# The samples' values of a cross-attention, with the probabilities as the stationary operand in four column groups

## The reference

```python
qh = q.reshape(bsz, t, H_C, DH_C)                 # 4 heads of 128
s = jnp.einsum('bthd,bmhd->bhtm', qh, mem_k) * (DH_C ** -0.5)
p = jax.nn.softmax(s, axis=-1)
o = jnp.einsum('bhtm,bmhd->bthd', p, mem_v).reshape(bsz, t, D_C)
y_c = o @ w_c_out
...
merged = g[:, :, 0] * y_a + g[:, :, 1] * y_b + g[:, :, 2] * y_c
```

## Time and profile before

| | us |
|---|---|
| median of 3 runs | 1988.23 (1987.68 to 1988.99) |
| the profiled execution | 1984.89 |
| its span, first to last instruction | 1983.1 |
| TensorE busy | 1878.6 |
| VectorE busy | 1482.1 |
| ScalarE busy | 1066.3 |
| GpSimd busy | 136.5 |

### The profile page before, as it was taken

The page is one execution under the profiler, slowest core; times in us unless marked ns, Lnnn a source line. Parts: engine busy times, 40 slices in busy tenths (PEclk is TensorE's granted clock), DMA queues, the critical chain, the costliest instruction groups (busy, mean ns, idle before and its releaser), DMA issues.

```text
span 1983.1 us, 28034 instructions
## 1 busy us (share of the span) xinstructions
PE 1878.6 (95%) x10353; PEld 1604.9 (81%) x10354; DVE 1482.1 (75%) x2119; ACT 1066.3 (54%) x1206; POOL 136.5 (7%) x159
## 2 busy tenths in 40 slices
PE   7999999899998999999889999999999999999993
PEld 7899899799987989899766678888888888886672
DVE  6997686755536999667576668888888888886665
ACT  4452754543324444474444456767777776765442
POOL 1110000000001020000020001020202020201000
PEclk9999999899999999999989999999999999999997
DMA  7553344344443563444456569898989898996522
GB/s 268 203 215 143 138 151 144 109 168 149 149 141 116 191 229 136 149 149 150 149 211 250 199 233 339 335 382 331 374 331 380 337 375 333 366 346 241 210 106 87
DMA packets 118613, 446.91 MB, mean 225 GB/s; under 512 B 10384, under 2 KB 10384, under 8 KB 118016
## 3 DMA queue, kind: packets, MB, share of 16 engines
q1 hardware_dynamic: 112288, 424.45, 58.1%
q0 software_dynamic: 6240, 21.33, 3.2%
HBM read 435.68 MB, written 12.67 MB: 226 GB/s over the span
## 4 chain that ended last, share of the span: by engine, by line
PE 42%; issue 3%; DVE 3%; ACT 1%; DMA 1%; SPq 0%; DVEq 0%; POOLq 0%; POOL 0%; ACTq 0%
PE psum L1996 11%; PE psum L1997 11%; PE psum L1998 11%; PE psum L2003 3%; PE psum L2002 3%; ACT wph L616 1%; PE psum L1736 1%; PE psum L2059 1%; DVE wpl L622 1%; DVE hT L1674 0%; DMA x<-out_acc 0%; DMA out_acc<-arena,rows_out 0%; DVE arena L1663 0%; PE psum L2062 0%; DVE x L1164 0%
## 5 line engine op out<-in xcount | busy, mean ns | idle before, releaser
L622 DVE TENSOR_TENSOR wpl<-e_ring,wph 128x2048 fp32r<-128x2048 f32 x269 | 606.9, 2289 | 85.5 <-ACT wph L616 84.5
L616 ACT CAST wph<-e_ring 128x2048 fp32r<-128x2048 f32 x269 | 501.7, 1903 | 119.6 <-PE psum L1998 66.7
L574 DVE TENSOR_TENSOR wl<-ring,wh 128x1024 fp32r<-128x1024 f32 x234 | 285.3, 1223 | 208.1 <-ACT wh L568 207.4
L1750 PE MATMUL psum<-xTh,wh 128*128 128x320 f32 x1184 | 375.3, 317 | 31.6 <-DVE xTl L1266 11.0
L1751 PE MATMUL psum<-xTl,wh 128*128 128x320 f32 x1184 | 369.9, 312 | 0.0
L1752 PE MATMUL psum<-xTh,wl 128*128 128x320 f32 x1184 | 369.7, 312 | 0.0
L568 ACT CAST wh<-ring 128x1024 fp32r<-128x1024 f32 x234 | 243.9, 1046 | 138.6 <-PE psum L1771 71.2
L1996 PE MATMUL psum<-wph,xe 128*128 128x512 f32 (+1 forms) x768 | 293.6, 382 | 2.8 <-issue 2.4
L1997 PE MATMUL psum<-wph,xe 128*128 128x512 f32 (+1 forms) x768 | 289.1, 376 | 0.0
L1998 PE MATMUL psum<-wpl,xe 128*128 128x512 f32 (+1 forms) x768 | 288.7, 376 | 0.0
L1750 PEld LDWEIGHTS psum<-xTh,wh 128*128 128x128 f32 x1184 | 225.7, 191 | 40.0 <-DVE wl L574 15.7
(11 more groups left out here) (327 smaller groups left out, 2528.5 us busy)
## 6 DMA issues: line engine op xcount, KB each, us to landing
e_ring<-experts SPq DMA_DIRECT2D x264, 1024.0 KB, 6.4
ring<-stream SPq DMA_DIRECT2D x274, 512.0 KB, 3.2
lnp<-rows POOLq DMA_DIRECT2D x4, 1024.0 KB, 6.1
x<-x POOLq DMA_DIRECT2D x3, 512.0 KB, 5.8
arena<-x0T SPq DMA_DIRECT2D x2, 640.0 KB, 5.9
o_a<-arena POOLq DMA_DIRECT2D x2, 540.0 KB, 7.6
o_k<-arena POOLq DMA_DIRECT2D x2, 512.0 KB, 7.0
o_v<-arena POOLq DMA_DIRECT2D x2, 512.0 KB, 8.8
```

The source lines that it names most:

```text
L574: dve.tensor_tensor(wl[:, q % SPLITS, :], ring[:, u % SLOTS, :], wh[:, q % SPLITS, :].bitcast(F32), ALU.subtract).then_inc(lo_done, 1)
L616: act.copy(wph[:, SLOT_OF[m % NPOS], :], ring_place(m).rearrange("p u c -> p (u c)")).then_inc(hi_e, 1)
L622: dve.tensor_tensor(wpl[:, s, :], ring_place(m).rearrange("p u c -> p (u c)"), wph[:, s, :].bitcast(F32), ALU.subtract).then_inc(lo_e, 1)
L1750: pe.matmul(out, h[:, k], hi[:, k], start=(k == 0), stop=False)
```

## The change

The values of four samples are made together. The stationary operand is now the 32 columns of probabilities of one sample (4 heads x 8 tokens) and the moving operand the 512 columns of its values; the four samples go to four groups of 32 partitions of one bank (`ob`). ScalarE copies that bank to SBUF (`obs`), and four transposes, one for each head, turn it into a bank `ot`, from which only the blocks on the diagonal (the head's own rows) are copied into `oTh` and subtracted into `oTl`. The four banks `o` now hold the prompt alone. A list `ATTEND` gives the order of the stretch: ob0, g0, g1, ot0, g2, g3, ob1, g4, mean, g5, ot1, g6, g7, var. The stream in memory is as before; `stands_at` tells where each unit stands in it.

```diff
-MEAN_AFTER = 2
+ATTEND = [("ob", 0), ("g", 2, 0), ("g", 2, 1), ("ot", 0), ("g", 2, 2), ("g", 2, 3), ("ob", 1), ("g", 2, 4),
+          ("mean", 0), ("g", 2, 5), ("ot", 1), ("g", 2, 6), ("g", 2, 7), ("var", 0)]
+MEAN_AFTER = 4
...
+        for n, key in enumerate(ATTEND):
+            p.tile(l, *key, bank=others[n % 4])
+        p.step([(l, "o", h) for h in range(H_C)])
+        for key in ATTEND:
+            if key[0] == "ob":
+                for n in range(4):
+                    p.step([(l, *key)] if n == 3 else [], (l, "cv", 4 * key[1] + n))
+            elif key[0] == "g":
+                p.step([(l, *key)], (l, *key), split=True)
+            else:
+                p.step([(l, *key)])
...
                 for n in range(H_C):
                     made(l, "o", n)
-                    act.copy(oTh[:, n], bank(l, "o", n)[:, 0:T]).then_inc(oh_ready, 1)
+                    act.copy(oTh[:, n, 0:SEQ], bank(l, "o", n)[:, 0:SEQ]).then_inc(oh_ready, 1)
+                for key in ATTEND:
+                    if key[0] == "ob":
+                        made(l, *key)
+                        frees(act.copy(obs[:, key[1]], bank(l, *key)), l, *key)
+                    elif key[0] == "ot":
+                        made(l, *key)
+                        act.copy(four_samples(oTh, key[1]), diagonal(bank(l, *key))).then_inc(oh_ready, 1)
+                    elif key[0] == "g":
+                        gates_of(2, key[2], None)
...
                 for n in range(KT):
                     split_at(l, "g", 2, n)
-                    if n in (0, 1, 5, 6):
-                        conv_b({0: 0, 1: 2, 5: 4, 6: 6}[n])
+                    if n == 3:
+                        samples_lo(0)
+                    if n in (0, 1, 2, 6):
+                        conv_b({0: 0, 1: 2, 2: 4, 6: 6}[n])
...
+                samples_lo(1)
...
+                def attend(q):
+
+                    four = range(4 * q, 4 * q + 4)
+                    w = [weights(pe, l, "cv", b).rearrange("p (m c) -> p m c", m=2) for b in four]
+                    take(pe, l, "ob", q)
+                    for m in range(2):
+                        for n, b in enumerate(four):
+                            c = 2 * P * m + 32 * b
+                            ins = product(bank(l, "ob", q)[32 * n:32 * n + 32, :], pT[:, H_C, c:c + 32], w[n][:, m], m, 2)
+                            if m:
+                                step(ins)
+
+                def samples_turned(q):
+
+                    emptied(pe, l, "ob", q)
+                    take(pe, l, "ot", q)
                     for h in range(H_C):
-                        for m in range(2):
-                            c = 2 * P * m + 32 * b + DSEQ * h
-                            ins = product(bank(l, "o", h)[:, SEQ + DSEQ * b:SEQ + DSEQ * b + DSEQ],
-                                          w[:, m, P * h:P * h + P], pT[:, H_C, c:c + DSEQ], m, 2)
+                        ins = pe.transpose(bank(l, "ot", q)[:, 120 * h:120 * h + P], obs[:, q, P * h:P * h + P], ident[:])
                     step(ins)
```

More of the change, by code:

```diff
@@ L239, in make_plan @@
         others = [(p.next_bank + n) % BANKS for n in range(4)]
-        p.tile(l, "mean", 0, bank=others[0])
+        for n, key in enumerate(ATTEND):
[9 more added lines that the diff above has]
+                p.step([(l, *key)])
+        first = p.unit_of[l, "cv", 0]
         for n in range(KT):
-            p.tile(l, "g", 2, n, bank=others[(n + 1) % 4])
-        p.tile(l, "var", 0, bank=others[(KT + 1) % 4])
+            p.stands_at[p.unit_of[l, "cv", n]] = first + 2 * n
+            p.stands_at[p.unit_of[l, "g", 2, n]] = first + 2 * n + 1
         for br, y in BRANCHES:
-            for n in range(KT):
-                if br == 2:
-                    p.step([(l, "o", h) for h in range(H_C)] if n == DEC - 1 else [], (l, "cv", n))
+            for n in range(KT if br != 2 else 0):
                 p.step([(l, "g", br, n)], (l, "g", br, n), split=True)
[L249 to L252, removed]
             for n in range(KT):
@@ L386, in trunk @@
         pp, mg = blocks_of(v, 10, N_MEM), blocks_of(v, KT, T)
+        obs = blocks_of(v, 2, D_C)
         merged = place("merged", [P, KT, 2 * T], arena_at + 4 * off[0], F32R)
@@ L584, in near, with four_samples, diagonal @@
                     u < sum(done <= step for done in plan.unit_done) + 2 * AHEAD)
+        def four_samples(v, q):
+            return v[:, :, SEQ + 32 * q:SEQ + 32 * q + 32].rearrange("p h (b t) -> p h b t", b=4)
+        def diagonal(bank_):
+            return bank_.rearrange("p (h b r) -> p h b r", h=H_C, b=4)[:, :, :, 0:DSEQ]
         def samp(v):
@@ L1379, in _, with samples_lo @@
                     tap(k)
+                def samples_lo(q):
+                    dve.wait_ge(oh_ready, (H_C + 2) * l + H_C + q + 1)
+                    frees(dve.tensor_tensor(four_samples(oTl, q), diagonal(bank(l, "ot", q)),
+                                            four_samples(oTh, q).bitcast(F32), ALU.subtract), l, "ot", q)
                 for n in range(KT):
                     split_at(l, "g", 2, n)
-                    if n in (0, 1, 5, 6):
-                        conv_b({0: 0, 1: 2, 5: 4, 6: 6}[n])
+                    if n == 3:
+                        samples_lo(0)
+                    if n in (0, 1, 2, 6):
+                        conv_b({0: 0, 1: 2, 2: 4, 6: 6}[n])
                     if n == MEAN_AFTER + 1:
@@ L1391, in _ @@
                 for n in range(H_C):
-                    dve.wait_ge(oh_ready, H_C * l + n + 1)
-                    frees(dve.tensor_tensor(oTl[:, n], bank(l, "o", n)[:, 0:T], oTh[:, n].bitcast(F32),
+                    dve.wait_ge(oh_ready, (H_C + 2) * l + n + 1)
+                    frees(dve.tensor_tensor(oTl[:, n, 0:SEQ], bank(l, "o", n)[:, 0:SEQ], oTh[:, n, 0:SEQ].bitcast(F32),
                                             ALU.subtract), l, "o", n)
+                samples_lo(1)
                 split_at(l, "yc", 1)
@@ L1862, in _ @@
                     emptied(pe, l, "v", m)
[L1863 to L1868, removed]
-                            for m in range(2):
-                                product(bank(l, "o", h)[:, 0:SEQ], vm[:, m, P * h:P * h + P],
-                                        pT[:, h, N_MEM * m:N_MEM * m + SEQ], m, 2)
+                for h in range(H_C):
+                    take(pe, l, "o", h)
+                    for m in range(2):
+                        ins = product(bank(l, "o", h)[:, 0:SEQ], vm[:, m, P * h:P * h + P],
+                                      pT[:, h, N_MEM * m:N_MEM * m + SEQ], m, 2)
@@ L1877, in attend @@
                     step(ins)
[L1880 to L1891, removed]
+                for key in ATTEND:
+                    if key[0] == "ob":
+                        attend(key[1])
+                    elif key[0] == "ot":
+                        samples_turned(key[1])
+                    elif key[0] == "g":
+                        blocks((l, *key), xTh, xTl, T)
+                    elif key[0] == "mean":
+                        pe.wait_ge(conv_a_tap, K_A * (l + 1))
+                        take(pe, l, "mean", 0)
+                        for j in range(JA):
+                            ins = product(bank(l, "mean", 0)[:, 0:T], ones[:], ca[:, j], j, JA)
+                        step(ins)
+                    else:
@@ L1896, in _ @@
                         step(ins)
+                for br, yk in BRANCHES:
+                    for n in range(KT if br != 2 else 0):
+                        blocks((l, "g", br, n), xTh, xTl, T)
                     if br == 1:
@@ L1904, in _ @@
                             emptied(pe, l, "o", h)
+                        for q in range(2):
+                            emptied(pe, l, "ot", q)
                     else:
```

3 lines of the change are left out of this document (removed).

## The result

The changed kernel takes 1972.23 us (median of 4 runs, 1969.8 to 1973.02) where the kernel before takes 1988.61 (4 runs): a ratio of 0.9914, interval 0.9897 to 0.9931, so it is 16.4 us faster. The forecast was 9.1 us faster, 1979.1 with a range from 1973 to 1985. The profiled execution took 1972.35 us, with a span of 1970.6 against 1983.1, 12.5 us less: the profiles differ by less than the medians do, which is the first thing to explain. Throughout, yc0 is the first tile of the projection behind the stretch, and a wait is time in which TensorE has nothing it may start.

The account below looks back on a forecast made before the run. VectorE was taken as the limit close behind TensorE: of 2 x 9.5 us of TensorE work and 7.4 of old stalls, nearly two thirds go to new waits and VectorE's end chain, leaving 9.1: 1988.23 becomes 1979.1, range 1973 to 1985.

Parts of the forecast that it names:

- What bounds the stretch: From cv0 to yc0: TensorE alone would save 9.5 us a layer, but VectorE, about three quarters busy, limits the gain.
- The walk: Engines followed in order through layer 0, carried to layer 1: yc0 earlier by 4.5 to 6.1 and 3.0 to 4.6 us; 69 in 100.
- The price of a wide group: Eight wide matmuls on TensorE (ob0, ob1) take 1.86 us, as the scores do; 7.0 us if the groups didn't overlap.
- A turn of transposes: Four transposes on TensorE turning a wide group's result, priced at 0.47 us, two turns a layer.
- The rival limit: Packing speeds up TensorE but not the emptying of PSUM, so copies may limit; the 9.5 us are not to be had.
- The load of g2: Into cv0's slot, free at 156.8, landing in 3.2 us, no slack; rival at 4.7 us gives 1982, 13 in 100.
- The half clock's rate: From g3 in layer 0: 3.4 us at half clock did 1.9 us of work, so a whole tile takes 6.3 us.
- the rival with half clock up to yc0: Clock stays at half from g4 to yc0 behind the new waits, 15.6 us a layer: 2009 us, 3 in 100.
- The clock fell behind one of the two stalls of before.: Before, the half clock cost 1.6 us once, in layer 0, behind the wait on the mean's bank; layer 1 had none.
- Behind yc0 the engines stand to each other as before, so the gain should last.: From yc0 on nothing further is won or lost, so the 9.1 us gained up to yc0 stay.
- the waits of before and their clock: TensorE's old stalls: 2.07 and 2.12 us ahead of g3, 0.81 twice ahead of yc0, 1.6 of clock; 7.4 us.

Follow-up runs that it names:

- e6: Kernel before with only the places moved (mean behind g4 instead of g2, third conv_b at g2), narrow matmuls kept: 1978.67 us against 1988.64, ratio 0.995.
- e3: Changed kernel with the low parts of the gate tiles in reach 6 units ahead instead of 4: 1976.78 us, ratio 0.9932 to the kernel before.
- e10: Changed kernel with one extra group of eight 32x512 matmuls behind ob1 in each layer, result unread: 1974.99 us, ratio 0.9929 to the kernel before.
- e2: Changed kernel with one extra group of eight 32x512 matmuls behind ob0 in each layer, result unread: 1978.27 us, ratio 0.9943 to the kernel before.
- e7: Changed kernel with gate tiles' low parts in reach 6 units ahead and the third conv_b moved from g2 to g4: 1967.11 us, ratio 0.9891.
- e8: Kernel of e7 with the third conv_b directly behind samples_lo(0) and the fourth behind the mean's square: 1963.96 us, ratio 0.9873 to the kernel before.

## Why the prediction was right on the side and wrong on the size

- **What bounds the stretch: right.** By the forecast's count TensorE's work fell by 9.5 us a layer. The fair comparison is the kernel with only the places moved (e6): beside it, yc0 came 1.8 us earlier in both layers together (the mean of two profiles). The waits up to yc0 grew from 0.81 to 6.4 and 6.5 us, and 10.2 us at half clock came where e6 has none.
- **The walk: within 1.3 us of what came.** It had g0 at 8.3, g4 at 28.2 and yc0 at 48.8 to 50.4 us behind the heads; two profiles have 8.8 to 8.9, 28.7 to 28.8 and 49.3 to 51.7. The 51.7 has 6.8 us at half clock behind g4, where the walk allowed for one fall of 3.4. The walk also looked for a fall behind g4 alone. In three of four cases one came behind g0; it cost nothing, since the wait ahead of g4 shrank by 1.3 to 1.5 us (from 3.17 us without a fall to 1.84 and 1.64 with one) and g4 started at 28.7 to 28.8 with it and without. The earlier low parts (e3) show that VectorE's chain sets g4, whatever TensorE does ahead of it.
- **The price of a wide group: right**, and a little high: from start to start it takes 1.74 us (177.03 to 178.77 in the kernel of e10), where 1.86 was taken from the scores. A turn of transposes takes 0.36 (169.51 to 169.87), not 0.47.
- **The rival limit.** The Trainium skill ("TensorEngine Tiling (Array Packing)", Performance Considerations, PSUM Bottleneck) cautions that the copies out of PSUM may become the limit. In the trace the limit did leave TensorE, but the copies are not what binds (`samples_lo` takes 0.28 us): it is where conv_b and the low parts stand.
- **The load of g2: it has little slack.** The rounding that waits for it started at 160.94, where 160.0 was forecast for the landing. VectorE idled 0.1 us for it, so most of g4's delay against the walk (0.55 us) is that the taps ended at 159.55 and not at 159.1. A landing 1 us later (e2) is passed on to g4.
- **The half clock's rate: right by luck.** The forecast's 1.9 us of work in 3.4 us should read 1.8 (3.52 - 1.7), which gives 6.6 us for a tile; by the matmuls' distance at half clock, 0.267 us (161.51 to 164.18 for ten), a tile takes 6.4. The clock came back behind each fall, so the rival with half clock up to yc0 is out.
- **Wrong: "The clock fell behind one of the two stalls of before."** I took what one execution showed as the rule, and priced the stall of before at 1.6 us of clock, once. The three other profiles have yc0 at 56.22 on average in layer 0 and 55.89 in layer 1, instead of 54.96 and 53.47: 3.7 us more that the change takes away. The clock still falls in the changed kernel, for 10.2 us in each of its two profiles against 10.2 to 13.6 in those three; but before, no wait behind the fall took it up: the one ahead of yc0 is 0.81 us with and without a fall. The sign was there in the forecast itself: the profiled execution was 3.3 us below the median, and I subtracted the gain from the median as if the 3.3 us lay outside the change.
- **Wrong: "Behind yc0 the engines stand to each other as before, so the gain should last."** ScalarE's copies of the heads now stand early, so the root's table is loaded before var ends (199.90), and VectorE's gated products of branch A come 9.43 us behind yc0 instead of 10.98 (212.26 - 202.83; 217.99 - 207.01). The waits of 0.31 and 1.01 us ahead of yc6 and rg went. yc0 to rg fell from 15.91 to 14.36 and 14.20: 3.3 us in both layers. Putting the copies back gave back half of it; the other half is argued, not shown.
- **The sum again.** 9.1 + 3.7 + 3.3, less 1.4 for a yc0 that was on average 0.7 us later than the walk's middle, is 14.7 us up to rg. The spans (1988.6 on average for three profiles, 1971.6 for two) differ by 17.0. The other 2.3 us are covered by the experts' stretch shown with e10, 2.7 us longer in three of the four profiles of before (at about 1190 us) than in the changed kernel's two. Why there is not shown; the forecast had nothing for it.
- **How the gain divides.** Moving the mean and conv_b alone (e6) gives 10 us. Of the other 7, in the profiles, 1.8 are at yc0, 3.3 lie between yc0 and rg, and 2.7 in the experts' stretch, where nothing was changed (in sum 1.2 us more than the spans differ by, 6.6). So the wide matmuls themselves have brought little so far; what they gave is room on TensorE, which e7 and e8 begin to use. The wide matmuls with the mean at its old place were not run. The forecast treated all of it as one and gave 7.4 us for the waits of before and their clock.

## What to carry to other kernels

When a second engine is three quarters busy in a stretch, price a change there by walking that engine's instructions in order, hand-over by hand-over; the walk here was within 1.3 us of g0, g4 and yc0. Take a stall's price, clock included, from several executions: one that lies below the median has left something out, and it may be just what the change removes. When TensorE waits for another engine, rearranging that engine's work is worth more than less work on TensorE: the same matmuls, with the low parts in reach earlier and conv_b at other places, gave 7.5 us more, and the mean moved by two tiles, with one conv_b moved too, gave 10 us with no matmul changed. And look where a half clock falls: behind g0, ahead of a wait that VectorE alone sets, it cost nothing here; behind g4 a fall of 3.4 us goes with a yc0 1.4 us later (50.79 against 49.34) and one of 6.8 us with 2.3 (51.74 against 49.44).

## What the runs showed of the hardware

- With a stall of TensorE of 2.1 to 2.6 us, at the same place of the same kernel, came a granted clock of 0.50 for 6.8 us in five of eight cases, for 3.4 us in two, and in one none. In the five the fall began while TensorE still stood, in the two about 1 us behind the stall.
- In the changed kernel a fall of 3.4 us behind g0 left the start of g4 where it was (28.7 to 28.8 us behind the heads), as g4 waits for VectorE.
- A group of eight fp32 matmuls with 32 stationary and 512 moving columns in four column groups (16 records) took 1.74 us from start to start; its records span 1.92 us, and 1.94 with the records of one column group in a row.
- Eight such matmuls more, put into a wait of TensorE, left the tiles behind the wait where they were (e10). With a load of the ring starting beside them, that load landed 1 us later and the tiles behind came later (e2); that the one caused the other is not shown.
